# Squared-ReLU MLP of a decoder step: fourteen up units by seven block products instead of eight, with the sums on VectorE and ScalarE

## The reference

```
x = x + g_a * (mixed @ w_out)
h2 = rms_norm(x, norm_mlp) * (1.0 + sc_m) + sh_m
x = x + g_m * (jnp.square(jax.nn.relu(h2 @ w_up)) @ w_down)
y = rms_norm(x, final_norm)
```

## Time and profile before

| | |
|---|---|
| median of 3 runs | 1152.51 us (1148.27 to 1153.26) |
| the profiled execution | 1152.23 us, its span 1150.4 us |
| mean granted clock of TensorE in it | 0.987 |
| MLP stage | from about 709 us to the end of the span |
| busy: TensorE, VectorE, ScalarE, GpSimd | 1099.8, 682.5, 487.3, 88.1 us |
| matmuls of line 847 on `hR` / on `actR` | 3744, busy 523.5 us / 1920, busy 260.9 us |

### The profile page before, as it was taken

How to read it: one execution, slowest core, us unless ns; L and a number is a source line. 1 busy time by engine, 2 the same in 40 slices (tenths; PEclk the granted TensorE clock), 3 DMA queues, 4 the chain that set the end, 5 groups by cost and what they waited for, 6 DMA issues and landing times.

```text
span 1150.4 us, 21500 instructions
## 1 busy us (share of the span) xinstructions
PE 1099.8 (96%) x8725; PEld 1041.6 (91%) x8725; DVE 682.5 (59%) x1512; ACT 487.3 (42%) x851; POOL 88.1 (8%) x65
## 2 busy tenths in 40 slices
PE   5899999998999999999999998899999999999997
PEld 4698889976999999999899998899999999999997
DVE  5736554444487877778875545637355563636465
ACT  3543556456544454643444224542323323242334
POOL 2400000000000000000000011420101001010101
PEclk9899999999999999999999999999999999999998
DMA  9884333212321313222222481222232223223202
GB/s 307 270 296 155 116 106 109 77 38 74 119 93 56 113 58 113 77 76 69 81 83 88 152 255 42 65 83 74 74 110 74 74 75 109 74 74 97 73 16 83
DMA packets 108775, 120.20 MB, mean 104 GB/s; under 512 B 2692, under 2 KB 98780, under 8 KB 108389
## 3 DMA queue, kind: packets, MB, share of 16 engines
q1 hardware_dynamic: 108677, 118.83, 32.2%
HBM read 108.99 MB, written 11.80 MB: 105 GB/s over the span
## 4 chain that ended last, share of the span: by engine, by line
PE 79%; DVE 11%; ACT 5%; issue 3%; DMA 1%; POOL 0%; SPq 0%; DVEq 0%; ACTq 0%; POOLq 0%
PE PS L847 59%; PE PS L802 4%; PE PS L956 2%; DVE wR L1403 2%; PE PS L820 2%; ACT wR L1086 1%; PE PS L793 1%; DVE xhat L1371 1%; PE PS L926 1%; PE PS L904 1%; PE PS L890 1%; ACT pr L1213 1%; DMA xn<-in_x_sample 1%; PE PS L769 1%; PE PS L996 1%
## 5 line engine op out<-in xcount | busy, mean ns | idle before, releaser
L847 PE MATMUL PS<-hR,wR 128*128 128x288 f32 x3744 | 523.5, 298 | 0.8 <-issue 0.8
L847 PEld LDWEIGHTS PS<-hR,wR 128*128 128x128 f32 x3744 | 502.7, 188 | 9.7 <-issue 8.8
L1403 DVE TENSOR_TENSOR wR<-raw,wR 128x512 fp32r<-128x512 f32 x260 | 203.1, 781 | 107.7 <-ACT wR L1086 100.2
L847 PE MATMUL PS<-actR,wR 128*128 128x288 f32 (+2 forms) x1920 | 260.9, 297 | 1.8 <-DVE actR L1545 1.8
L847 PEld LDWEIGHTS PS<-actR,wR 128*128 128x128 f32 x1920 | 257.0, 189 | 3.0 <-DVE actR L1545 2.0
L1086 ACT ACTIVATE wR<-raw 128x512 fp32r<-128x512 f32 x260 | 164.4, 632 | 140.6 <-PE PS L847 132.9
L1465 DVE CAST actR<-tmp 128x576 fp32r<-128x576 f32 x32 | 15.2, 476 | 125.8 <-ACT tmp L1197 125.8
L802 PE MATMUL PS<-wR,hR 128*128 128x256 f32 x600 | 77.5, 286 | 0.0
L802 PEld LDWEIGHTS PS<-wR,hR 128*128 128x128 f32 x600 | 73.4, 191 | 1.8 <-issue 1.7
L1420 DVE SCALAR_TENSOR_TENSOR xT<-PS,mods,xT 128x288 f32<-128x288 f32 x68 | 35.2, 518 | 62.8 <-PE PS L847 56.2
L1196 ACT ACTIVATE tmp<-PS 128x576 f32<-128x576 f32 x32 | 20.9, 652 | 120.0 <-PE PS L847 117.7
(11 more groups left out here) (219 smaller groups left out, 1066.1 us busy)
## 6 DMA issues: line engine op xcount, KB each, us to landing
raw<-in_w_in SPq DMA_DIRECT2D x30, 1024.0 KB, 5.2
raw<-in_w_up SPq DMA_DIRECT2D x16, 1024.0 KB, 5.4
raw<-in_w_down SPq DMA_DIRECT2D x16, 1024.0 KB, 5.1
mid<-in_w_ada SPq DMA_DIRECT2D x12, 1024.0 KB, 5.2
ada<-in_w_ada SPq DMA_DIRECT2D x8, 1024.0 KB, 12.0
S<-in_state_hgrn SPq DMA_DIRECT2D x8, 512.0 KB, 4.4
out_hgrn_sample<-S SPq DMA_DIRECT2D x8, 512.0 KB, 6.7
raw<-in_w_out SPq DMA_DIRECT2D x4, 1024.0 KB, 5.6
```

Source lines behind the costliest of these rows:

```text
L847: mm = pe.matmul(PS[:, 2 * x.pair + h, 0:size], weights(x, w, k, col), rhs[r], start=(k == 0 and n == 0), stop=(k == last and n == 2))
L1403: done(dve.tensor_tensor(w[:, 1, cols], raw[SLOT[SPLITS[n]]][:, cols], w[:, 0, cols].bitcast(F32), ALU.subtract), s_lo)
```

## The change

A product of 2 x 2 blocks is made with seven block products instead of eight. For up units 2 to 15 (`SEVEN`) the unit's weights are cut into four blocks (two groups of 128 columns by two halves of the rows; "21" is the second column group, first row half), the input h2 into four (row half, token half). TensorE's products, in order, are `PRODUCTS`: weight block or sum, token block or sum, bank, and whether the bank starts anew. Each has 4 row blocks x 3 = 12 matmuls of 288 columns.

- The four sums of tokens (T1 to T4) are made once, on VectorE (`combine`, in up 0), and split into high and low parts (`halve`, in up 1) into `tR`; the input in float32 stays in `xhat1` for that, in place of the four `tmp` buffers.
- The four sums of weights (S1 to S4) are made for each unit on VectorE (`sums`) in `tmp2` and `tmp3`. A unit is then prepared in seven pieces of 512 columns (`PIECES`) instead of four; TensorE waits for the piece of each product instead of for the whole unit.
- Three of a unit's banks hold partial results. ScalarE copies four of them out (`seven`, 288 columns each), where the next product adds into the same bank; VectorE makes three sums; ScalarE then does relu, square and the high part for the first tile in the unit itself and for the second at the start of the next unit (`relu`, `squares_of`). GpSimd makes the low parts (`low`). Even and odd units have result buffers of their own (`KEPT`), and their own bank for the first products.

```diff
+SEVEN = [u for u, x in enumerate(UNITS) if x[0] == "up" and x[1] >= 2]
+PRODUCTS = [("11", "11", 0, True), ("12", "21", 1, True), ("S2", "T2", 0, False), ("S1", "T1", 2, True),
+            ("S3", "T3", 0, False), ("S4", "22", 2, False), ("22", "T4", 0, False)]
+PIECES = ["11", "12", "S1", "S3", "S2", "22", "S4"]
...
+            at_ = x.n * parts(x) + c
+            if squared is not None and at_ == 0:
+                yield ("low", squared, 0)
+            elif squared is not None and at_ == 2:
+                yield ("low", squared, 1)
+                squared = None
...
+            if x.kind == "up" and x.i == 0 and x.n == 0 and c == 3:
+                yield ("combine",)
+            if x.kind == "up" and x.i == 1 and x.n == 0:
+                yield ("halve", c)
+            if x.u in SEVEN:
+                yield ("seven", x, c)
+            if squared is not None and at_ == 0:
+                yield ("relu", squared)
+            elif squared is not None and at_ == 1:
+                yield ("squared", squared)
...
-            if at < 4 and (x.kind, x.i) != ("up", 0) and x.split + 1 < len(SPLITS):
+            if (x.kind, x.i) != ("up", 0) and x.split + 1 < len(SPLITS) and at < CUTS[x.split + 1]:
...
-        levels = sb("levels", [P, MASK], U8)
...
+        KEPT = [tmp[0:2], [rb, kept1]]
...
+            def product(x, c):
+
+                j = SEVEN.index(x.u)
+                wa, tb, i, start = PRODUCTS[c]
+                bank = bank_of(x, i)
+                pe.wait_ge(s_lo, cuts(x.split, PIECES.index(wa) + 1))
...
+                if c == 0:
+                    if j >= 2:
+                        pe.wait_ge(s_freed, j - 1)
+                elif c == 1:
+                    if j:
+                        pe.wait_ge(s_added, 3 * j - 2)
+                elif c == 3:
+                    if j:
+                        pe.wait_ge(s_added, 3 * j)
+                else:
+                    pe.wait_ge(s_kept, 4 * j + {2: 1, 4: 2, 5: 3, 6: 4}[c])
...
+                    for n, (l, r) in enumerate(((0, 0), (0, 1), (1, 0))):
+                        mm = pe.matmul(bank[:, 0:HALF], w[l], t[r], start=(start and k == 0 and n == 0), stop=(k == 3 and n == 2), skip_group_check=True)
...
+            def seven(x, c):
+
+                j = SEVEN.index(x.u)
+                if c == 1:
+                    return
+                if c == 5:
+                    act.wait_ge(s_added, 3 * j + 3)
+                    done(act.activation(kept(x, 0)[:], kept(x, 0)[:], ACT.Relu))
+                    squares_of(x, 0)
+                    return
+                if c == 6:
+                    return
+                bank = bank_of(x, PRODUCTS[c][2])
+                act.wait_ge(s_prod, 6 * j + c + 1)
+                if j == 0:
+                    act.wait_ge(s_alo, 2 * x.i)
...
+                done(act.activation(halves_of(x, dst[0])[dst[1]], bank[:, 0:HALF], ACT.Copy), s_kept)
...
+            def sums(n, q):
...
+                if q == 0:
+                    dve.wait_ge(s_raw[SLOT[u]], raw_loads(u))
+                    done(dve.tensor_tensor(one, cut(w, "21"), cut(w, "22"), ALU.add), s_sum)
+                    done(dve.tensor_tensor(three, cut(w, "11"), cut(w, "21"), ALU.subtract), s_sum)
+                elif q == 3:
+                    done(dve.tensor_tensor(one, one, cut(w, "11"), ALU.subtract), s_sum)
+                elif q == 5:
+                    done(dve.tensor_tensor(one, cut(w, "12"), one, ALU.subtract), s_sum)
+
+            def seven(x, c):
...
+                elif c == 5:
+                    dve.wait_ge(s_kept, 4 * j + 4)
+                    first_, second = halves_of(x, 1)
+                    done(dve.tensor_tensor(second, second, first_, ALU.add), s_added)
...
+                done(dve.tensor_tensor(to, to, add, ALU.add), s_added)
```

More of the change, by code:

```diff
@@ L352, in walk @@
                 scanning = None if c else scanning
+        if x.u in SEVEN:
+            if x.n:
+                squared = x
+            continue
         if turning:
@@ L436, in stage @@
             st, out = ExitStack(), []
-            for name, shape in tensors:
-                out.append(sb(name, shape, F32, st))
+            for name, shape, *dt in tensors:
+                out.append(sb(name, shape, *(dt or [F32]), st))
             st.close()
@@ L572, in decay, with cut, columns, summed @@
             return G[r % 2][:, DECAY[m]:DECAY[m] + w // m].rearrange("p (a two) -> p a two", two=2)
+        def cut(t, b):
+            k, m = 4 * (int(b[1]) - 1), P * (int(b[0]) - 1)
+            return t.rearrange("p (k c) -> p k c", c=UC)[:, k:k + 4, m:m + P]
+        def columns(t):
+            return t[:, 0:4 * P].rearrange("p (k c) -> p k c", c=P)
+        def summed(b):
+            return tmp[2 if b == "S3" else 3]
+        def piece(n, b):
+            u = SPLITS[n]
+            w = wR[split_index(n)]
+            if b in WX:
+                dst = [columns(wX[n % 2][WX.index(b)][:, part, :]) for part in range(2)]
+            else:
+                dst = [cut(w[:, part, :], "21" if b == "S1" else b) for part in range(2)]
+            return (columns(summed(b)) if b[0] == "S" else cut(raw[SLOT[u]][:], b)), dst
+        def bank_of(x, i):
+            return A[(0 if x.i % 2 == 0 else 3) if i == 0 else i]
+        def tokens_of(b):
+            k, h = 4 * (int(b[0]) - 1), int(b[1]) - 1
+            return xhat1[:, k:k + 4, h * HALF:(h + 1) * HALF]
+        def combined(b):
+            return tF[:, TX.index(b), 1, :].rearrange("p (k c) -> p k c", c=HALF)
+        def kept(x, n):
+            return KEPT[x.i % 2][n]
+        def halves_of(x, n):
+            return kept(x, n)[:, 0:HALF], kept(x, n)[:, HALF:TOK]
         def act_tile(x):
@@ L1298, in _ @@
                     last_squares(*x)
+                elif ev == "halve":
+                    halve(*x)
+                elif ev == "seven":
+                    seven(*x)
+                elif ev == "squared":
+                    squares_of(x[0], 1)
+                elif ev == "relu":
+                    relu(*x)
                 elif ev == "final":
@@ new lines, in halve @@
+            def halve(c):
+                dve.wait_ge(s_thi, c + 1)
+                done(dve.tensor_tensor(tR[:, c, 1, :], tF[:, c, 1, :], tR[:, c, 0, :].bitcast(F32), ALU.subtract), s_tlo)
+            def sums(n, q):
+                u = SPLITS[n]
+                w = raw[SLOT[u]][:]
+                one, three = columns(summed("S1")), columns(summed("S3"))
+                if q == 0:
[6 more added lines that the diff above has]
+                    done(dve.tensor_tensor(one, cut(w, "12"), one, ALU.subtract), s_sum)
@@ L1682, in _ @@
                     merge(*x)
+                elif ev == "combine":
+                    combine(*x)
+                elif ev == "halve":
+                    halve(*x)
+                elif ev == "seven":
+                    seven(*x)
                 elif ev == "y_put":
@@ L1743, in _ @@
                     modulate(*x)
+                elif ev == "low":
+                    low(*x)
                 elif ev == "evac":
```

128 lines of the change are left out of this document (113 added, 15 removed).

## The result

| | before | after |
|---|---|---|
| median of the runs | 1151.02 us (4 runs) | 1167.47 us (1163.5 to 1168.28, 4 runs) |
| ratio, 95% interval | | 1.0147 [1.0127, 1.0167] |
| span of the profiled execution | 1150.4 | 1165.7 |
| TensorE's matmuls | 8725 | 8557 |

The change makes the kernel 1.5% slower, 16.5 us. The forecast was 1168.7, in a range of 1147 to 1177.

What follows compares the result with a forecast made beforehand. TensorE, busy 96% of the span, was taken to bound the kernel. From 1152.23 us, -22.3 + 13.3 + 11.2 + 1.2 + 10.8 + 2.3 = +16.5 gave 1168.7 us, range 1147 to 1177.

Steps and rivals of the forecast that it cites:

- first pair, A to C: From the start of up unit 2 to the first down unit behind its pair: +11.8 us against before.
- each of six pairs, A to C: From a later pair's first up unit to the first down unit behind it: -1.3 us each against before.
- each C and D: The two down units behind each pair of up units: +1.8 us against before.
- The saving: Up units 2 to 15 run seven products for eight, 1.59 us less each: -22.3 us.
- B's stalls: Second up unit of each pair: third and fifth products wait for ScalarE's copies, two stalls of 0.95, +13.3 us.
- C's stall: First down unit behind each pair: third tile waits for VectorE's residual behind a late weight piece, 1.6 x 7, +11.2 us.
- D's 0.2: Second down unit behind each pair: extra sums make the second residual 0.2 us late, 6 x 0.2, +1.2 us.
- The start: Up unit 2: its third product waits for a copy held by unit 1's low part, +10.8 us.
- The clock: Behind unit 2's long wait the clock falls; 24 matmuls take 5.74 us for 3.45, +2.3 us.
- rival 3: The clock falls at the stalls of every pair too: 7 x 2.3 more, 1184.8 us; chance 0.04.
- Rival 1: The other engines' queues keep up and only the start is lost: 1143.0 us, or 1137; chance 0.16.

Runs made afterwards that it cites:

- the version without stalls in the pairs: The change with result buffers exchanged, ScalarE's work on up units' first tiles moved into the next unit, weight pieces first in down units: 1140.04 us, ratio 0.9912.

## Why the prediction was right

The stage can be added up from TensorE's start of unit 2 to the last ordinary down unit. By the prediction's terms and by the trace:

| stretch | predicted against before | in the trace |
|---|---|---|
| first pair, A to C | -3.2 + 1.9 + 10.8 + 2.3 = +11.8 | 36.97 - 25.44 = +11.5 |
| each of six pairs, A to C | -3.2 + 1.9 = -1.3 | 24.20 - 25.44 = -1.24 |
| each C and D | 1.6 + 0.2 = +1.8 | 27.37 - 25.60 = +1.8 |

11.5 - 6 x 1.24 + 6 x 1.8, with 1.4 for the last stretch before the final units (36.55 us from its C at 1095.01 to 1131.56, 35.14 before), is +16.3 us; the median rose by 16.5. The two profiled spans differ by 15.3: unit 1 began 1.4 us earlier, which is scatter, and the end took 0.3 longer.

- *The saving* is real: 1.60 us a product, and in the version without stalls in the pairs a pair takes 22.31 us for 25.44, 3.13 of the 3.18.
- *B's stalls* were put at 0.95 each. The listed waits are 0.70, but a pair takes 24.20 us for the 22.31 without stalls, 0.95 a stall: TensorE loses another 0.2 beyond the idle time that the profile names. Copy begun: 14.73 forecast, 827.29 - 812.64 = 14.65 measured. The run with A's first tile later shows the cause by taking it away. The order of the queues is the one forecast, VectorE's half of S2's piece ahead of its two sums, ScalarE's five instructions ahead of the copy.
- *C's stall* was put at 1.6, and is 1.31 (once 1.66) plus 0.12. The chain was the right one by time (GpSimd at 4.49 for 4.6 after C's start, the piece's end at 6.47 for 6.65). That GpSimd holds it is shown by the run with GpSimd held back, which also shows that this part alone is worth little; that ScalarE's order is what counts is shown by the run with the pieces first.
- *D's* 0.2, a term for which the prediction shows no working, was 0.35, and it goes with the weight sums (19.19 us for 19.54). The list of waits and TensorE's matmul row are silent on it; only the weight loads' row in the timeline has it:

```profile
809.36 3.21 PEld L982 LDWEIGHTS PS<-actR,wR 128*128 128x128 f32 x24 [0.32 <-DVE tmp_s L1668]
```

- *The start* was put at 10.8, with the low part of unit 1's second tile as the last in the chain: 10.56, and ScalarE waited 2.66 us for just that:

```profile
761.62 0.41 ACT L1258 ACTIVATE tmp<-PS 128x288 f32<-128x288 f32 x1 [2.66 <-POOL actR L1992]
```

  That the size fits is in part luck. From unit 2's start the cast ended at 759.53 - 748.30 = 11.23 us where 761.4 - 749.65 = 11.75 had been worked out, and GpSimd's low part took 1.84 for 1.45; the two errors cancel. VectorE's half of S2 ended 6.75 after that start, where 8.35 had been worked out. And the prediction missed that the queue was nearly as late by itself, so that taking the buffer away gave 2.7 us and not most of it.
- *The clock*: 2.3 forecast from another idle time, 2.1 measured; the short waits leave it at 1.00, which refutes rival 3 for this kernel. The stretches (us, busy (x) of PE, PEld, DVE, ACT, POOL, granted clock, DMA):

```profile
737.00:778.00 41.00, 29.74 (x208) 29.34 (x207) 31.84 (x37) 22.58 (x35) 9.18 (x5) 0.88 0.12 44
778.00:830.00 52.00, 49.17 (x365) 48.30 (x364) 37.60 (x69) 26.21 (x45) 5.72 (x4) 1.00 0.26 82
```

  The rule of the Trainium skill beside rival 3 ("TensorE: Matmul & The Clock Gate", A second HAM failure mode) speaks of frequent short idles around banks; three in 51.6 us, of 0.7 to 1.7 us, did nothing to the clock in this kernel. Only behind the long wait does a product take 3.02 us for 1.60, as at the lower of the two levels. But rival 3 was nearer than this trace alone says: with waits of 2.5 us in C, in the run with A's first tile later, the clock did fall three times in seven. The prediction's ground, an idle of 1.55 us at 1.00, covered the stalls that came and none much longer.
- *Rival 1* named the right lever. It needed ScalarE's chain between P6 and the next unit's copy to be 0.9 us shorter. The chain did not shorten by itself, nor by overlap of activations, which the Trainium skill ("ScalarE: Activation LUTs", What ACT_TABLE_LOAD costs) puts at some 93 ns: the three in a row at 823.80, 824.52 and 825.24 start 0.72 apart with 0.69 each, no overlap. Each of them waits for its predecessor's end here; no run has them without that wait. The chain did shorten by order, to 1140.04, close to the rival's 1143.

## What to carry to other kernels

When work is taken off the busiest engine and given to engines with room, cost the chain between two of its instructions, not their sum of work: here 67% and 50% went with 1140.04 us in one order and with 1167.47 in another (2.7 of these 27 us are the exchanged buffers). An instruction that frees something for the bottleneck belongs ahead of everything in its queue that only prepares the future. And a repair is judged by the list of waits before the time: in three of these runs (A's first tile later, the copy moved up, GpSimd held back) a wait was cured and came back, in whole or in part, further on. Read the matmuls behind a wait too: their length tells whether the clock fell.

## What was not expected of the hardware

- A wait of TensorE costs more than its idle time. In the second group B begins at 823.80 and P3 is due at 827.00, 3.20 later; it starts at 827.84, 0.84 late with a listed idle time of 0.72, and P4 only 1.68 us behind it where 1.60 is usual. So 0.92 is lost for 0.72 listed, and the last group reads the same (1081.97, 1086.01, 1087.68). The 0.92 is read from starts; the listed idle time rests on the modelled end of the matmul before it, so part of the gap may be the model's.
- GpSimd's and VectorE's instructions took longer beside one another in unit 1 of the change: GpSimd's low parts took 1.84 us there, where they take 1.42 in the pairs, and VectorE's 512-column sums beside them 1.77 for 0.69.

```profile
754.47 1.84 POOL L1992 TENSOR_TENSOR actR<-tmp,actR 128x576 fp32r<-128x576 f32 x1 [9.73 <-DVE actR L1711]
755.09 1.77 DVE L1633 TENSOR_TENSOR tmp<-raw,tmp 128x512 f32<-128x512 f32 x1
```
